# Moving attention's bias table out of the head of the scan stage, and loading u in two pieces

## The reference, cut to what matters

```python
def rel_bias(dist, table):              # shared T5 bias of attention, 32 buckets, 8 heads
    b = table[rel_bucket(dist)].astype(jnp.float32)
    b = jnp.moveaxis(b, -1, 0)
    return b.reshape((N_KV_HEADS, GQA) + dist.shape)

def s5_scan(u, lam_re, ...):            # 32 groups of 16 channels, complex state of 64
    bu = jnp.einsum('blgc,gpc->lbgp', u32.astype(jnp.complex64), bbar)
    _, h = lax.associative_scan(combine, (a, bu), axis=0)
    y = jnp.einsum('lbgp,gcp->blgc', h, cmat).real
    y = y + d_skip * u32
```

## Time and profile before

| | us |
|---|---|
| median of 3 runs | 1509.99 |
| lowest and highest run | 1506.92, 1511.5 |
| span of the profiled execution (no other time of it is given) | 1510.9 |

### The profile page before, as it was taken

How to read it: one execution, slowest core, us unless ns; L and a number is a source line. 1 busy time by engine, 2 the same in 40 slices (tenths; PEclk the granted TensorE clock), 3 DMA queues, 4 the chain that set the end, 5 groups by cost and what they waited for, 6 DMA issues and landing times. The chain is left out here.

```text
span 1510.9 us, 24472 instructions
## 1 busy us (share of the span) xinstructions
PE 1330.7 (88%) x7142; PEld 1037.1 (69%) x7142; DVE 1153.1 (76%) x2083; ACT 816.8 (54%) x1683; POOL 650.9 (43%) x730
## 2 busy tenths in 40 slices
PE   5999999989897889699999997389999999999930
PEld 2688888856575556487777775178888788888820
DVE  3888888836675777556666665789999999999936
ACT  2433332303345668434444442278888888888844
POOL 1107766732224860012111121257666577657625
PEclk9999999979999999799999998599999999999975
DMA  9423444489995552324444435766888988885779
GB/s 329 137 86 149 169 157 156 161 278 337 301 307 154 174 181 90 130 85 149 159 154 156 147 126 176 254 206 130 232 236 243 271 223 244 244 222 139 216 232 357
DMA packets 138447, 298.25 MB, mean 197 GB/s; under 512 B 22244, under 2 KB 79717, under 8 KB 135886
## 3 DMA queue, kind: packets, MB, share of 16 engines
q1 hardware_dynamic: 110550, 218.63, 42.2%
q0 software_dynamic: 20800, 61.13, 17.4%
q10 hardware_dynamic: 7024, 17.60, 3.3%
HBM read 305.18 MB, written 102.25 MB: 270 GB/s over the span
## 5 line engine op out<-in xcount | busy, mean ns | idle before, releaser
L2809 DVE TENSOR_TENSOR ex_w_lo<-route_wgu,ex_w_hi 128x1024 fp32r<-128x1024 f32 x192 | 225.6, 1217 | 4.4 <-ACT ex_w_hi L2620 3.7
L2620 ACT ACTIVATE ex_w_hi<-route_wgu 128x1024 fp32r (+1 forms) x192 | 193.4, 1069 | 2.4 <-issue 2.3
L147 PE MATMUL ex_ps_h<-ex_w_hi,ex_xT 128*128 128x512 f32 x384 | 156.5, 408 | 6.5 <-DVE ex_x_lo L2838 6.2
L2579 POOL DMA_INDIRECT scratch_acc<-route_o,ex_to x48 | 96.2, 2004 | 152.7 <-ACT route_o L2647 75.3
L149 PE MATMUL ex_ps_h<-ex_w_hi,ex_x_lo 128*128 128x512 f32 x384 | 151.7, 395 | 0.0
L148 PE MATMUL ex_ps_h<-ex_w_lo,ex_xT 128*128 128x512 f32 x384 | 150.7, 392 | 0.0
L2028 POOL TENSOR_SCALAR mx_st<-mx_st 128x1 f32<-128x1 f32 x68 | 29.4, 433 | 259.7 <-ACT mx_j L2072 151.8
L147 PE MATMUL fr_ps_m<-fr_whi,fr_hl 128*128 128x512 f32 (+1 forms) x384 | 138.7, 361 | 0.9 <-DVE fr_wlo L658 0.5
L149 PE MATMUL fr_ps_m<-fr_whi,fr_hl 128*128 128x512 f32 (+1 forms) x384 | 136.1, 354 | 0.0
L148 PE MATMUL fr_ps_m<-fr_wlo,fr_hl 128*128 128x512 f32 (+1 forms) x384 | 135.9, 354 | 0.0
L2846 DVE TENSOR_TENSOR ex_wd_lo<-route_wd,ex_wd_hi 128x1024 fp32r<-128x1024 f32 x96 | 114.1, 1229 | 6.9 <-ACT ex_wd_hi L2638 4.7
(11 more groups left out here) (503 smaller groups left out, 3484.5 us busy)
## 6 DMA issues: line engine op xcount, KB each, us to landing
route_wgu<-in_w_exp_gate_dram SPq DMA_DIRECT2D x48, 1024.0 KB, 12.8
route_wgu<-in_w_exp_up_dram SPq DMA_DIRECT2D x48, 1024.0 KB, 15.3
route_wd<-in_w_exp_down_dram SPq DMA_DIRECT2D x48, 1024.0 KB, 10.6
scratch_rec<-fr_w SPq DMA_DIRECT2D x16, 1112.0 KB, 4.2
s_rec<-scratch_rec SPq DMA_DIRECT2D x32, 556.0 KB, 6.0
scratch_proj<-fr_io SPq DMA_DIRECT2D x16, 640.0 KB, 3.0
scratch_acc<-in_zeros_dram SPq DMA_DIRECT2D x18, 512.0 KB, 5.7
fr_w<-in_w_ada_dram SPq DMA_DIRECT2D x8, 1024.0 KB, 8.0
```

What stands on the lines that cost most here:

```text
L147: nc.tensor.matmul(out, hi, w_hi, start=first, stop=False)
L2579: pool.indirect_dma_start(T["acc"], bass.IndirectOffsetOnAxis(to[:, t:t + 1], 0), o[:, t % 2, :], None, compute_op=ALU.add).then_inc(sem(" ...
L2620: A(w_hi[:, par, c * PW:(c + 1) * PW], wgu[:, bass.ds(slot * (KD * 2 * DE) + c * PW, PW)], ACT.Copy).then_inc(S["w_rounded"], 1)
L2809: vec.tensor_tensor(w_lo[:, par, c * PW:(c + 1) * PW], wgu[:, bass.ds(slot * (KD * 2 * DE) + c * PW, PW)], w_hi[:, par, c * PW:(c + 1) * P ...
```

## The change

The bias's eight matmuls ahead of the groups become 16 of 192 columns, one in each of the groups 2 to 17, on PE ahead of the product T of `back`. They write the free columns 264 to 455 of `ps_v`. ACT moves each piece out behind `out`, where DVE did it before. PE waits for the move of the last piece ahead of each next one. DVE widens the table behind scan(0) and turn(2).

On SP, u's first half-quarter is the first transfer. The bias's two tables come behind record 2. u's three other quarters become one load of two transfers (1.5 MB each, pieces of 1536 bytes) at the place of the second quarter. The store of the bias moves from ahead of record 4 to behind record 22, the load of it from behind record 14 to behind record 25.

```diff
+    def part(self, g):
+        n = g - self.FIRST
+        return (n // 2, slice(n % 2 * BW // 2, (n % 2 + 1) * BW // 2)) if 0 <= n < 2 * NH else None
+
+    def spread(self, nc, pe, g):
+        n = g - self.FIRST
+        if n == 0:
+            pe.wait_ge(self.widened, 1)
+        if 1 <= n <= 2 * NH:
+            pe.wait_ge(self.moved, n)
+        if self.part(g):
+            h, c = self.part(g)
+            nc.tensor.matmul(self.bank[:, NCH + DB:NCH + DB + BW // 2], self.wide[:, h, :], self.hot[:, c], start=True, stop=True)
+
+    def move(self, nc, g):
+        if self.part(g):
+            h, c = self.part(g)
+            nc.scalar.activation(self.rows[:, h, c], self.bank[:, NCH + DB:NCH + DB + BW // 2], ACT.Copy).then_inc(self.moved, 1)
...
-            def load_u(b):
-                c = slice(b * CB, (b + 1) * CB)
+            def load_u_rest():
                 for i in range(2):
-                    sp.dma_start(u[:, i, :, c], up[:, i, :, c]).then_inc(u_in[b], 16)
+                    sp.dma_start(u[:, i, :, CB:], up[:, i, :, CB:]).then_inc(u_rest, 16)
...
-            bias.load(sp, T)
+            sp.dma_start(u[:, 0, :, 0:CB], up[:, 0, :, 0:CB]).then_inc(u_first, 16)
             sp.dma_start(ident[:, :], T["ident"]).then_inc(loaded, 16)
-            sp.dma_start(u[:, 0, :, 0:CB], up[:, 0, :, 0:CB]).then_inc(u_in[0], 16)
             sp.dma_start(us[:, :, :], usv).then_inc(loaded, 16)
...
             load_rec(2)
+            bias.load(sp, T)
             load_rec(3)
             load_w(0)
-            load_u(1)
+            load_u_rest()
             load_w(1)
-            bias.store(sp, T, bias_out)
             sp.dma_start(T["cT"], cT[:, :, :].rearrange("p k n -> p (k n)")).then_inc(cT_out, 16)
             for g in range(U5, NG):
                 load_rec(g)
-                if g == 6 or g == 11:
-                    load_u(2 + (g == 11))
                 if g % 2 and g // 2 < NUNIT:
                     load_w(g // 2)
-                if g == 14:
+                if g == 22:
+                    bias.store(sp, T, bias_out)
+                if g == 25:
                     sp.wait_ge(bias_out, 16)
                     first.load_bias(sp, T)
...
                 C(yT[:, g % 2, :], ps_v[:, 0:NCH + DB], ACT.Copy).then_inc(yT_ready, 1)
+                bias.move(nc, g)
...
         def _(pe):
-            bias.spread(nc, pe)
             pe.wait_ge(loaded, 2 * 16)
...
                     pe.wait_ge(yT_ready, g)
+                bias.spread(nc, pe, g)
                 nc.tensor.matmul(ps_v[:, 0:NCH + DB], R(q, "T"), uT[:, q, :], start=True, stop=False)
...
-            bias.widen_and_move(nc, dve)
...
                     turn(g + 2)
+                if g == 0:
+                    bias.widen(nc, dve)
```

More of the change, by code:

```diff
@@ L965, with __init__ @@
 class AttentionBias:
-    def __init__(self, s, banks):
+    FIRST = 2
+    def __init__(self, s, bank):
         self.tab, self.wide, self.hot = s.sb("tab", [NBUCKET + 1, NH]), s.sb("wide", [NBUCKET + 1, NH, P]), s.sb("hot", [NBUCKET + 1, BW])
-        self.rows, self.banks = s.sb("rows", [P, NH, BW]), banks
-        self.loaded, self.masked, self.widened, self.done, self.moved = (s.sem(n) for n in ("tab_loaded", "masked", "widened", "bias_done", "bias_moved"))
+        self.rows, self.bank = s.sb("rows", [P, NH, BW]), bank
+        self.loaded, self.masked, self.widened, self.moved = (s.sem(n) for n in ("tab_loaded", "masked", "widened", "bias_moved"))
     def load(self, sp, T):
@@ L979, in store, with widen @@
     def store(self, sp, T, stored):
-        sp.wait_ge(self.moved, NH)
+        sp.wait_ge(self.moved, 2 * NH)
         sp.dma_start(T["bias_rows"], self.rows[:, :, :].rearrange("p h m -> p (h m)")).then_inc(stored, 16)
-    def widen_and_move(self, nc, dve):
+    def widen(self, nc, dve):
         nc.vector.memset(self.tab[NBUCKET:NBUCKET + 1, :], MASKED).then_inc(self.masked, 1)
@@ L1094, in s5 @@
         rec_in = [s.sem(f"rec{q}") for q in range(U5)]
-        u_in = [s.sem(f"u_in{q}") for q in range(4)]
+        u_first, u_rest = s.sem("u_first"), s.sem("u_rest")
         ug_ready, flipped, uT_ready = s.sem("ug_ready"), s.sem("flipped"), s.sem("uT_ready")
@@ L1102, in s5 @@
             [s.sem("w0"), s.sem("w1")], s.sem("mod_mm"), s.sem("mod_done"), s.sem("cleared"), s.sem("consts"), s.sem("folded"))
-        bias = AttentionBias(s, (ps_f, ps_y))
+        bias = AttentionBias(s, ps_v)
         blk = s.block()
@@ L1138, in store_y @@
                 res.store_y(sp, T, b)
-            bias.load(sp, T)
+            sp.dma_start(u[:, 0, :, 0:CB], up[:, 0, :, 0:CB]).then_inc(u_first, 16)
             sp.dma_start(ident[:, :], T["ident"]).then_inc(loaded, 16)
-            sp.dma_start(u[:, 0, :, 0:CB], up[:, 0, :, 0:CB]).then_inc(u_in[0], 16)
             sp.dma_start(us[:, :, :], usv).then_inc(loaded, 16)
             sp.wait_ge(proj_stored, (NT // 2 + 1) * 16)
-            sp.dma_start(u[:, 1, :, 0:CB], up[:, 1, :, 0:CB]).then_inc(u_in[0], 16)
+            sp.dma_start(u[:, 1, :, 0:CB], up[:, 1, :, 0:CB]).then_inc(u_first, 16)
             load_rec(0)
@@ L1186, in gather @@
                     act.wait_ge(flipped, g - U5 + 1)
-                if g % 8 == 0:
-                    act.wait_ge(u_in[g // 8], 32)
+                if g == 0:
+                    act.wait_ge(u_first, 32)
+                if g == 8:
+                    act.wait_ge(u_rest, 32)
                 C(ug[:, q, 0:2, :].rearrange("p i (j c) -> p i j c", j=L), u[:, :, :, cols(g)], ACT.Copy).then_inc(ug_ready, 1)
@@ L1257, in unflip @@
                 pe.wait_ge(yT_ready, g + 1)
-                pe.wait_ge(*((y_out, g) if g else (bias.moved, NH)))
+                if g:
+                    pe.wait_ge(y_out, g)
                 for i in range(2):
@@ L1273, in modulate @@
                 pe.wait_ge(w_in[n % 2], n // 2 * 16 + 16)
-                if n == 0:
-                    pe.wait_ge(bias.moved, NH)
                 if n == KD:
```

## The result

The changed kernel takes 1522.1 us (median of 9 executions, 1516.7 to 1528.6) against 1510.0 for the kernel before. The ratio is 1.0086, with a 95% interval of 1.0066 to 1.0107: slower by 10 to 16 us. A second series of it gave 1520.0 us and a ratio of 1.0066 (1.0033 to 1.0098). The forecast was 1509.1 us, with 1503.8 to 1514.6 as its range.

A forecast was written before the change was run, and what follows sets the result against it. PE's work and the queue of records were taken as close bounds up to about 400 us. 0 + 1.6 + 4.0 - 7.1 + 0.6 = -0.9 from 1510.9 gave 1510.0, forecast as a 1509.1 us median, range 1503.8 to 1514.6.

The forecast's parts named there:

- The head: Start of the scan stage: without the bias work and with u earlier, the first flip comes 4.0 us earlier.
- What is next: At contribute(4): record 4 lands at 348.3 us again, PE waits 3.5 to 5 us, the head's gain is spent; change 0.
- The clock behind the stall: After the wait at contribute(4): PE's clock falls to 0.50 for some 3.2 us, costing +1.6 us.
- The pieces: Fifteen bias matmul pieces behind contribute(4), 0.32 us each, partly filling PE's wait for POOL: +4.0 us, between 3.2 and 4.8.
- The queue later: Lags behind u's later quarters and the bias load vanish, 7.8 us, with 0.7 of stall kept at y's store: -7.1 us.
- The bias's transfers in groups 22 to 26: Moved store and load of the bias: store delays record 23 slightly, record 26 lands in time; +0.6 us, bounds 0 to 6.1.
- the rival's 6.1: Groups 21 to 24: bias store and load hold up records 23 and 26, 6.1 us instead of 0.6; chance 0.12.
- the sign that I had set for being wrong: Stated test of the forecast: it is wrong if gaps near records 23 to 27 exceed 3 us.
- three costs: Low clock after the wait at contribute(4) +1.6, bias pieces in the groups +4.0, late bias transfers +0.6 us.
- one gain of 7 us: Lags removed from the queue after group 4, as u's later quarters and the bias load leave: -7.1 us.
- the third: Rival: bias store and load hold up records 23 and 26 in groups 21 to 24, 6.1 us, total 1514.6; chance 0.12.
- the fourth: Rival: PE waits for ACT's moves of the bias pieces in each group, +4.8 us, 1513.9 or more; chance 0.04.

The follow-up runs named there:

- e1: The changed kernel with u loaded in quarters again, at the places of the kernel before; 1519.2 us, ratio to before 1.0053.
- e4: The kernel before with only u's second to fourth quarters made one load at the second's place; 1516.8 us, ratio to before 1.0038.
- e8: The changed kernel with the rest of u issued by ACT on its own queue instead of SP's; 1518.2 us, ratio to before 1.0050.
- e2: The changed kernel with the bias's weights and one-hot matrix zero-padded from 33 to 128 rows; 1516.6 us, ratio to before 1.0044.
- e3: The changed kernel with the bias's store and load moved behind record 31, the end of the stage; 1521.6 us, ratio to before 1.0064.
- e12: The kernel before, bias stored behind record 16, loaded per head behind records 20 to 27, u's later quarters behind records 4 and 8; 1508.4 us, ratio 0.9989.

## Why the prediction was wrong

**The head** was right to a few tenths: in the means the first flip comes 4.0 us earlier, and nothing of it is kept.

**"What is next"** was right in mechanism and place. The forecast had record 4 at 348.3 us; the stage began 0.74 us earlier in the changed profile, so 347.6, and contribute(4) starts at 347.27. e1, e4 and e8 each show the cause. Record 4's 0.2 us of slack belongs to the first profile, though. In the other three of the kernel before, group 2 comes 1.1 to 1.4 us sooner and PE waits for record 4 already, 1.88, 1.84 and 0.70 us, the first of them:

```profile
349.64 0.68 PE L1242 MATMUL s_ps_s<-s_uT,s_rec 128*128 128x264 f32 x2 [1.88 <-issue]
```

In part the landing was luck. The queue was to start 1.2 us earlier, but the rest of u is issued 9.06 us behind the first transfer, where the second quarter was issued at 8.90: the bias's tables still stand ahead of it, only behind record 2. The price of u's pieces had no row before; the rows now have one. Packets and queue 1 of 335 to 339 us of the changed kernel:

```profile
DMA packets 1063, 1.61 MB, mean 402 GB/s; under 512 B 16, under 2 KB 1063, under 8 KB 1063
q1 hardware_dynamic: 1063, 1.61, 106.6%
```

Nearly all are pieces of 1536 bytes: 4 us x 16 engines x 1.066 over 1063 is 64 ns each, where I took 69 between 59 and 88; over 2048 pieces on 16 engines that is 0.6 us less, which hides half of the missing lead. The range of 341 to 425 GB/s that the Trainium skill (DMA: Bandwidth & Descriptors, Measured) has for growing sizes holds this stretch's 402 GB/s as well; the page has it for transfers that GpSimd issues, these are SP's.

**The clock behind the stall** was under-sized: +1.6, from a low stretch of 3.2 us. In the first profile the stretch began inside the wait and lasted more than 8 us of work, which at half the clock is some 4. In the four profiles the groups 3 and 4 lose 4.3, 1.8, 4.7 and 3.5 us beyond the regular 8.38 and the gap, 3.6 in the mean. One of the four is what I had forecast. I had carried over the length of one earlier event as if it were a property of the chip. That is 2 of the 12 us.

**The pieces** were under-sized: +4.0, between 3.2 and 4.8. I priced 192 columns by the distance of two products of 128 rows. Measured is 0.42 to 0.52 us each, 0.94 a pair against a regular 7.44, so 7.0 us over the fifteen that I counted. Neither bound held it, because neither came from a row in which 33 rows stand between 128. I wrote that the weights load beside other work; the piece's own do, but T's behind it stood still for 0.23 us. e2 shows that the rows are the difference: padded, a piece costs 0.27 us, 4.1 over fifteen, which is my price. The 0.1 of POOL's wait per pair that I took off is visible (0.42 in odd groups against 0.52 in even ones), so that part was right. The step was 3 us too low.

**The queue later**: the lags of the kernel before went as forecast. Between groups 4 and 17 only one of 1.1 us remains, near group 12. In the four profiles of the kernel before these lags average less than in the first (54.4 us for the stretch against 55.7 in the profile that I read), so 1.3 us of the gain was never there on average. And 1.4 us of lag are left in the mean of the four changed ones, where I kept 0.7. Together that is 2 of the 12 us.

**"The bias's transfers in groups 22 to 26", +0.6**, is the step that failed most. It measured +5.9 for the stretch, which is the rival's 6.1, given a chance of 0.12. e3 shows it, and the sign that I had set for being wrong (gaps over 3 us near records 23 to 27) came: 4.3 us at 23, 26 and 27. I had summed the bytes in the queue against the time until record 23 is needed. Landing was to be 15.1 us behind the output of group 17; it was 17.1 (414.98 to 432.1). Missing in that sum was the time of the issues: the store and the two transfers of cache values stand between records 22 and 23, 2.55 us from 422.25 to 424.80, and record 23 entered the queue 2.7 us behind output 19. In e3 it entered 1.8 us behind output 19, and there was no gap; the rest came with the store. Record 22 was counted as on time. It was held by y's store (a gap of 0.59 us in e3 too), and with the bias's store issued behind it by as much again (1.23). Each gap costs PE its refill besides. For the load at record 25 I had counted 1 us of lateness and a landing in time; record 26 was issued 2.2 us late and landed 5.8 us later. Record 27 was issued only 0.4 us behind output 23 and took 9.2 us to land, behind late record 26 and 640 KB of attention's `held_qk`; neither stood in the sum. How much of the 6 us the store has and how much the load was not tested apart.

The forecast's sum was near zero because it set three costs against one gain of 7 us; all three costs were too low and the gain too high. Of the rivals only the third held one of the three. None held a longer low clock, and the fourth's 4.8 us were for waits for ACT's moves, which did not occur. The range stood on single rivals. The third and fourth together would have given 1519.4 us, near the result, but the fourth's part of it by luck.

## What to carry to other kernels

When a start is brought forward, find the next thing that the path needs and its own landing time first: with 0.2 us of slack at record 4 in the profile that was read, and none in three others, four microseconds at the head were worth nothing by group 3. Read more than one profile before a sum rests on a slack of tenths. Transfers on a queue that feeds a loop are priced twice, by the bytes ahead of the next record and by the issues ahead of it in the issuing engine, and the bias's store and load, moved to a quieter stretch, cost 6 us there; spread one by one, the loads cost little (e12). Here a matmul slipped in between others was cheaper with their number of rows.

## What the runs showed of the hardware

A product of 33 rows between products of 128 rows cost 0.2 us more than the same product padded with zeros to 128 rows, which is seen as a weight load behind it that stood still for 0.23 us, and did not with padding. The granted clock stayed at 0.50 for 3 us after one gap of 2.5 us, and for about 10.2, 3.4, 10.2 and 6.8 us around the same gap of one kernel in four profiles (3.93, 4.33, 4.43 and 4.11 us), with PE busy all the time behind it. A transfer on ACT's queue shared the engines with SP's, and record 4 passed it: u took up to 30.8 us to land instead of 16.8, and PE's gap at contribute(4) was gone.
